# Scores of the attention as three one-pass products of high and low parts, made one head pair ahead

## The reference, cut to what matters

```
def forgetting_attention(h, k, v, F, w_qg, q_gain, w_o):
    qg = h @ w_qg
    q, gate = qg[..., :D_MODEL], qg[..., D_MODEL:]
    q = rms_norm(split_heads(q), q_gain).transpose(0, 2, 1, 3)
    ...
        s = jnp.einsum('bhqd,bhkd->bhqk', qb, k).astype(jnp.float32) * sm_scale
        s = s + Fq[..., :, None] - F[..., None, :]
        s = jnp.where(kpos[None, :] <= qpos[:, None], s, -jnp.inf)
        p = jax.nn.softmax(s, axis=-1)
        return jnp.einsum('bhqk,bhkd->bhqd', p, v)
    ...
    return (o * jax.nn.sigmoid(gate)) @ w_o
```

## Time and profile before

| | us |
|---|---|
| median of 3 runs | 2545.86 |
| lowest and highest | 2544.88, 2550.26 |
| profiled execution, its own time | 2549.13 |
| its span, first to last instruction | 2547.3 |

### The profile page before, as it was taken

How to read it: one execution, slowest core, us unless ns; L and a number is a source line. 1 busy time by engine, 2 the same in 40 slices (tenths; PEclk the granted TensorE clock), 3 DMA queues, 4 the chain that set the end, 5 groups by cost and what they waited for, 6 DMA issues and landing times. The chain is left out here.

```text
span 2547.3 us, 36273 instructions
## 1 busy us (share of the span) xinstructions
PE 2452.7 (96%) x14664; PEld 1925.6 (76%) x14664; DVE 1245.2 (49%) x1849; ACT 743.6 (29%) x1439; POOL 1536.1 (60%) x784
## 2 busy tenths in 40 slices
PE   5999988999999999999999999999999999999998
PEld 4777766788888777667888877888775478787886
DVE  7647257775562244454444437877485643121112
ACT  5744423331120212543311212333324431111210
POOL 6874717677777776016988873533262067754774
PEclk9999999999999999999999999999999999999999
DMA  7322436566652222104656522323334273311221
GB/s 276 108 83 80 121 97 264 211 243 231 231 215 93 99 90 99 40 18 142 228 206 229 214 100 95 117 116 116 151 138 147 102 303 126 114 66 67 83 99 66
DMA packets 90334, 358.28 MB, mean 141 GB/s; under 512 B 27337, under 2 KB 41289, under 8 KB 52946
## 3 DMA queue, kind: packets, MB, share of 16 engines
q1 hardware_dynamic: 65712, 229.79, 24.9%
q10 hardware_dynamic: 24482, 126.50, 13.1%
HBM read 317.18 MB, written 39.06 MB: 140 GB/s over the span
## 5 line engine op out<-in xcount | busy, mean ns | idle before, releaser
L530 POOL TENSOR_TENSOR whi<-wraw,con_sb 128x512 fp32r<-128x512 f32 (+1 forms) x305 | 622.0, 2059 | 826.8 <-PE ps L586 606.5
L534 POOL TENSOR_TENSOR wlo<-wraw,whi 128x512 fp32r<-128x512 f32 (+1 forms) x305 | 796.4, 2632 | 12.9
L586 PE MATMUL ps<-hh,whi 128*128 128x512 f32 x936 | 365.7, 391 | 0.0
L586 PE MATMUL ps<-hh,wlo 128*128 128x512 f32 x936 | 364.2, 389 | 0.0
L586 PE MATMUL ps<-hl,whi 128*128 128x512 f32 x936 | 364.2, 389 | 0.0
L586 PEld LDWEIGHTS ps<-hh,whi 128*128 128x128 f32 x936 | 175.7, 188 | 41.0 <-issue 4.3
L586 PEld LDWEIGHTS ps<-hh,wlo 128*128 128x128 f32 x936 | 175.7, 188 | 36.7
L586 PEld LDWEIGHTS ps<-hl,whi 128*128 128x128 f32 x936 | 175.7, 188 | 35.9
L586 PE MATMUL ps<-midh,whi 128*128 128x512 f32 x512 | 199.7, 390 | 0.0
L586 PE MATMUL ps<-midh,wlo 128*128 128x512 f32 x512 | 199.2, 389 | 0.0
L586 PE MATMUL ps<-midl,whi 128*128 128x512 f32 x512 | 199.2, 389 | 0.0
(11 more groups left out here) (518 smaller groups left out, 4618.5 us busy)
## 6 DMA issues: line engine op xcount, KB each, us to landing
wraw<-wst SPq DMA_DIRECT2D x162, 1024.0 KB, 4.8
cond_w<-wcond ACTq DMA_DIRECT2D x68, 1024.0 KB, 4.8
first_w<-wcond SPq DMA_DIRECT2D x8, 1024.0 KB, 14.0
mod_w<-wcond SPq DMA_DIRECT2D x8, 1024.0 KB, 13.4
d_v<-key_and_query ACTq DMA_DIRECT2D x4, 1536.0 KB, 5.4
d_s<-ssb ACTq DMA_DIRECT2D x4, 1536.0 KB, 5.2
sld<-d_s SPq DMA_DIRECT2D x4, 1536.0 KB, 6.3
vld<-d_v SPq DMA_DIRECT2D x16, 384.0 KB, 3.5
```

The source lines that it names most:

```text
L530: o = pool.tensor_tensor(whi[:, s, c], wraw[:, f, c], C("zero").broadcast_to([P, width]), ALU.add)
L534: o = pool.tensor_tensor(wlo[:, s, c], wraw[:, f, c], whi[:, s, c].bitcast(F32), ALU.subtract)
L586: o = e.matmul(ps[:, b, :nt], w[:, k, mc], x[:, k0 + k, t0:t0 + nt], start=first and k == 0 and j == 0, stop=final and k == nk - 1 and j == 2)
```

## The change

Behind the norms, ACT rounds q and k of a pair to fp32r (`round_qk`, into `qk_high`, two pairs deep), and DVE subtracts the high from the whole and writes the low part over q and k, as `oh[:, i]` and `ol[:, i]` (`low_qk`). The scores are then three one-pass products per head, high q with high k, high q with low k, low q with high k, with the two heads alternating. Low with low is left out. The scores of a pair's first step now wait for the low parts (`qk_parted`). On ACT the two roundings stand behind the fourth and the fifth item of the pair before; on DVE the norm of k moves one step ahead, the low parts stand behind the maxima of the widest tile, and the low part of the output moves behind the next maxima.

```diff
@@ -2509,6 +2509,7 @@
         otile = tiles("otile", 25, shape=[P, T])
         pr, ptr = tiles("pr", 64, 4), [tiles(f"ptr{b}", 8 + 4 * b, 4) for b in range(4)]
         oh, ol = tiles("oh", 48, KT, F32R), tiles("ol", 32, KT, F32R)
+        qk_high = tiles("qk_high", 70, 4, F32R)
         sums = fixed("sums", [P, 4, 2, 4])
         top = fixed("top", [P, 4])
         NI, NS = 8 * KT, 4 * KT
@@ -2522,6 +2523,7 @@
             squared, summed = [signal("q_squared"), signal("k_squared")], [signal("q_summed"), signal("k_summed")]
             rooted, inverted, root_high = signal("qk_rooted"), signal("qk_inverted"), signal("root_high")
             gain_spread, pair_normed = signal("scale_spread"), signal("qk_normed")
+            qk_rounded, qk_parted = signal("qk_rounded"), signal("qk_parted")
             scored, topped, raised = signal("scores"), signal("max_ready"), signal("exp_done")
             turned, copied, totalled = signal("p_turned"), signal("p_copied"), signal("values_done")
             inverse, spread = signal("sum_inverse"), signal("sum_spread")
@@ -2579,16 +2581,17 @@
                 def scores(s):
                     i, t = s // 4, s % 4
                     if t == 0:
-                        pe.wait_ge(*pair_normed.at(2 * i + 2))
+                        pe.wait_ge(*qk_parted.at(2 * i + 2))
                     if s >= 2:
                         pe.wait_ge(*raised.at(2 * s - 2))
                     else:
                         pe.wait_ge(*g_read.at(2 * s + 6))
                     w = P * (t + 1)
-                    for h in range(2):
-                        rr = slice(64 * h, 64 * h + 64)
-                        pe.matmul(ps[:, score_bank(2 * s + h), :w], q_sb[rr, i, P * t:P * t + P], kk_sb[rr, i, :w], start=True,
-                                  stop=False)
+                    high, at = qk_high[:, 2 * (i % 2):2 * (i % 2) + 2], slice(P * t, P * t + P)
+                    for n, (q, k) in enumerate(((high[:, 0], high[:, 1]), (high[:, 0], ol[:, i]), (oh[:, i], high[:, 1]))):
+                        for h in range(2):
+                            rr = slice(64 * h, 64 * h + 64)
+                            pe.matmul(ps[:, score_bank(2 * s + h), :w], q[rr, at], k[rr, :w], start=n == 0, stop=False)
                     for h in range(2):
                         to = ps[:, score_bank(2 * s + h)]
                         pe.matmul(to[:, :w], pick_r[:, 2 * i + h:2 * i + h + 1].broadcast_to([P, P]), f_split[:, 0, :w],
@@ -2703,6 +2706,12 @@
                                    ps[:, turn_bank(n), :P * (t + 1)].rearrange("p (s t) -> p s t", t=P),
                                    ACT.Copy).then_inc(*copied.inc())
 
+                def round_qk(i, j):
+                    act.wait_ge(*pair_normed.at(2 * i + j + 1))
+                    if i >= 2:
+                        act.wait_ge(*scored.at(8 * i - 8))
+                    act.activation(qk_high[:, 2 * (i % 2) + j], (q_sb, kk_sb)[j][:, i], ACT.Copy).then_inc(*qk_rounded.inc())
+
                 def round_of(i):
                     act.wait_ge(*weighted.at(i + 1))
                     act.activation(oh[:, i], otile[:], ACT.Copy).then_inc(*rounded.inc())
@@ -2729,6 +2738,9 @@
                 root_of(0)
                 for k in range(KT):
                     read_g(k)
+                    if k == 5:
+                        round_qk(0, 0)
+                        round_qk(0, 1)
                 fold_read_out(act, 11, 4)
                 exp(0)
                 exp(1)
@@ -2738,6 +2750,8 @@
                         exp(n + 2)
                     if n % 8 == 3 and n > 8:
                         round_of(n // 8 - 1)
+                    if n % 8 in (3, 4) and n // 8 + 1 < KT:
+                        round_qk(n // 8 + 1, n % 8 - 3)
                 round_of(KT - 1)
                 squares_of_x(act, x_squared, x_added, 5)
                 qk_read_out(act, 12, 4)
@@ -2759,6 +2773,11 @@
                     dve.wait_ge(*gain_spread.at(2 * i + j + 1))
                     dve.scalar_tensor_tensor(x[:, i], x[:, i], gain, ps[:, VALUES if j else SPREAD], ALU.mult,
                                              ALU.mult).then_inc(*pair_normed.inc())
+
+                def low_qk(i, j):
+                    dve.wait_ge(*qk_rounded.at(2 * i + j + 1))
+                    dve.tensor_tensor((oh, ol)[j][:, i], (q_sb, kk_sb)[j][:, i], qk_high[:, 2 * (i % 2) + j].bitcast(F32),
+                                      ALU.subtract).then_inc(*qk_parted.inc())
 
                 def maximum(n):
                     w = P * (item(n)[2] + 1)
@@ -2804,14 +2823,14 @@
                 low_of(0)
                 norm(0, 0)
                 norm(0, 1)
+                low_qk(0, 0)
+                low_qk(0, 1)
                 maximum(0)
                 maximum(1)
                 for s in range(NS):
                     i, t = s // 4, s % 4
                     if t == 0 and i:
                         sum_inverse_of(i - 1)
-                    if t == 2 and i + 1 < KT:
-                        norm(i + 1, 1)
                     if s + 1 < NS:
                         maximum(2 * s + 2)
                         maximum(2 * s + 3)
@@ -2820,7 +2839,11 @@
                         weigh(i - 1)
                     elif t == 1 and i + 1 < KT:
                         norm(i + 1, 0)
-                    if t == 2 and i:
+                        norm(i + 1, 1)
+                    elif t == 2 and i + 1 < KT:
+                        low_qk(i + 1, 0)
+                        low_qk(i + 1, 1)
+                    if t == 3 and i:
                         part(i - 1)
                 sum_inverse_of(KT - 1)
                 gate(KT - 1)
```

## The result

The changed kernel took 2581.54 us (median of 4 runs, 2579.26 to 2582.78), the kernel before in the same sessions 2548.06 (2544.88 to 2550.63): ratio 1.0128, 95% interval 1.0116 to 1.0140, or 33 us slower. The prediction was 2572, slower.

What follows compares the result with a forecast made beforehand. PE was taken to bound the loop, except around the last two exponentials, where ACT does. Wait and groups +14.2 us plus clock falls +12.3 made +26.5, 2572 us against the median; range 2554 to 2588.

Steps and rivals of the forecast that it cites:

- The heads already run side by side, order is worth nothing: Score products on PE: both heads already overlap in different halves of the array's rows, so alternating them gains nothing.
- The groups: Both heads' score products per 128 queries: 0.52, 0.57, 0.72, 0.90 us at 128 to 512 keys, about -0.27 us per pair.
- The wait: PE idles 2.8 us before the next pair's scores, for DVE's low part of k behind ACT's rounding; period +2.15 us.
- without the clock: +14.2: Whole kernel at full clock: seven longer periods between pairs, +15.0 us, less 0.8 given back outside them.
- The clock: Granted clock falls behind four in five of seven holes between pairs: 5.6 falls at 2.2 us, +12.3 us.
- the 14 to 17 us: Sign expected in the later trace: a head pair's period of 14 to 17 us instead of 12.34.
- The predicted 26.5: Whole kernel: 14.2 us without the clock plus 12.3 us for its falls, +26.5 us.
- the clock did not stay: Rival for the loop: same wait, but holes leave the clock up; +14 us, 2560; chance 0.22.
- the heads do overlap in fp32r: Rival for score products, that heads do not overlap in fp32r: some 1.2 us per pair more, about 2582; chance 0.10.
- the wait was not covered: Rival before a pair's scores, that k's low part is ready in time: -2.2 us, 2543.7; chance 0.13.
- the fixed part of a group did not vanish: Rival for score groups, wait covered and each group's fixed 0.21 us gone: -9 us, 2537; chance 0.05.

Runs made afterwards that it cites:

- the heads in turn: Kernel before with three one-pass score products on the first pair's parts for every pair, one head's three then the other's; 2550.71 us, ratio 0.9997.
- the products alone: Kernel before with three one-pass score products, heads alternating, only the first pair rounded and parted and used for every pair; 2548.65 us, ratio 0.9996.
- the hole filled: Changed kernel with 11 unread products of 512 columns in front of each later pair's wait for low parts; 2564.31 us, ratio 1.0061.
- half filled: Changed kernel with five unread products of 512 columns in front of each later pair's wait for low parts; 2570.44 us, ratio 1.0078.
- rounding of k earlier: Changed kernel with ACT's rounding of k right behind that of q, ahead of the third tile's copy; 2572.97 us, ratio 1.0095.
- parts and wait alone: Changed kernel with roundings, low parts and wait kept, but scores still fp32 products and low parts unread; 2579.71 us, ratio 1.0112.

## Why the prediction was right, and where its size was off

*The heads already run side by side, order is worth nothing.* Right: 11.97 and 11.99 us with the heads alternating and in turn, records in pairs in both. The rule of the Trainium skill that I had weighed against the rows ("TensorE: Matmul & The Clock Gate", Part 3, The mechanism), strict program order, would have asked for about 0.4 us more (an estimate) in each 512 group with the heads in turn, had they reached PE so; no run here shows it. If the compiler alternates the heads, the rule itself was not tested.

*The groups.* Foretold 0.52, 0.57, 0.72 and 0.90 us, measured 0.48, 0.55, 0.72 and 0.89 in the products alone. The gain per pair was 0.37 instead of 0.27; the groups make up 0.32 of it.

*The wait.* Foretold a hole of 2.8 us, released by DVE's low part of k, which waits for ACT's rounding; measured 2.60, with that chain (2.17 in the first pair). The period at full clock was to be 14.49 us and is 14.37 with the hole filled. The term "without the clock: +14.2" measured +14 in the loop (117.7 against 103.7 us) and +15 in the time. A part of the 14 is not the wait: the fall in the first pair lasted 6.8 us with the hole filled and 3.4 us before. What that is worth shows from the loop's start to the first spread sums, in two couples of traces where only this fall sets them apart: 19.63 us with the hole filled (6.8) and 18.40 half filled (3.4), 17.68 with the heads in turn (6.8) and 16.51 with the products alone (3.4), so 1.2 us both times. Both lengths came in kernels with the wait and without it, so I don't put this to the change. The wait is then about 14.0 - 1.2 = 12.8 us, 1.4 less than I had charged: half of that lies in the six full periods (2.03 us longer each, not 2.15), the rest mostly in the first pair with its shorter hole. The two runs that move ACT's rounding (one step: hole 1.64; out of the string: none) show the cause, and that the roundings' cost is their place.

*The clock.* Here the size was off. I charged 5.6 falls at 2.2 us, +12.3. The loop of the changed kernel is 137.8 - 117.7 = 20.1 us longer than with the hole filled, both with a fall of 6.8 us in the first pair. The number was too small, since all seven holes had a fall, and so was the price: 20.1 / 7 = 2.9 us. The falls came in three lengths, about 3.4, 6.8 and 10.2 us, and against the 14.37 us of a pair at full clock they cost 1.1 (15.46), 2.8 (17.15) and 4.2 us (18.54), mean 2.7 over the six pairs shown; the seventh, behind the first hole, was of the longest and cost 4.0. The windows of the earlier trace rows held only the first two lengths, two and two; here the longest came three times in seven. The pairs with it, 18.54 and 18.56 us, lie outside the 14 to 17 us that I had given for the period. Of the shortfall, length times one minus clock (1.7, 3.4 and 5.1 us), two thirds to four fifths reached the time: PE is bound by itself for most of what follows the hole.

The sum, corrected: 13 for the wait, 20 for the clock and 1 for the longer fall in the first pair are 34 us, against 33.5 between the medians. The predicted 26.5 lacked 8 of the clock, and 1.4 too much in the wait hid a part of that. Against the measured 2581.54 the number 2572 is 9 us short: 7 in the change, and 2 because the median of before in the same sessions is 2548.06 and not the 2545.86 that I started from. The rivals fell one by one: the clock did not stay, the heads do overlap in fp32r, the wait was not covered, and the fixed part of a group did not vanish (0.89 - 3 x 0.23 = 0.20 us).

## What to carry to other kernels

Room in an engine's sum is not room at a place in its queue: 1.1 us of copies on an engine idle for a third of the time cost 2 us per round, since they stood in the one stretch where that engine's string led to PE's next piece; the same copies in its own hole cost nothing. Before adding a wait to PE, find what releases it, follow that engine's queue back, and look for the pair of rows where it has been idle. And where PE gets a hole that returns every 12 to 18 us, count the clock with it: more than half of this loss was not the hole but the half clock that came with it, and filling the hole with useless products won 17 us.

## What the runs showed of the hardware

In the fallen stretches the granted clock is 0.50, so 1.2 GHz instead of 2.4. One program, with the same hole in each pair, had a fall at some of its holes and none at others. Counted in one trace for each kernel, the holes that come back with every pair, by their length:

| idle of PE, us | holes | with a fall | kernel |
|---|---|---|---|
| 0.39 | 7 | 0 | before |
| 1.01 | 1 | 0 | hole half filled, first pair |
| 1.45 | 6 | 5 | hole half filled |
| 1.58 | 1 | 0 | rounding of k earlier, first pair |
| 1.64 | 6 | 3 | rounding of k earlier |
| 2.17 | 2 | 1 | changed (fall), parts and wait alone (none), first pair |
| 2.43 | 6 | 6 | parts and wait alone |
| 2.60 | 6 | 6 | changed |

Between 1.45 and 1.64 us the share does not grow with the length, and so few holes are too little to say more. The waits of the last pair (0.92, 0.39 and 0.69 us in a row) stand in every trace and had a fall in one of ten. The three falls of 10.2 us in the changed kernel began half a microsecond before their holes ended, the four shorter ones about 1.4 us behind the end of theirs. What decides between a fall and none, and on its length, these runs leave open.
